# Two attention stages of a fused two-block kernel: heads taken in pairs on TensorE, and a longer distance between the steps of a head

## The reference

```
# latent attention (layer 0), 8 heads, q and k of 64+32 = 96 numbers, v of 64
s = (einsum('bhqd,bhkd->bhqk', qn, k_nope) + einsum('bhqr,bkr->bhqk', qr, k_rope)) * scale
p = softmax(s);  o = einsum('bhqk,bhke->bhqe', p, v)
# neighbourhood attention (layer 1), 16 heads, q, k, v of 64
s = einsum('bhcd,bhicjd->bhcij', q_row, k_win) * scale + bias
p = softmax(s);  o = einsum('bhcij,bhicje->bhce', p, v_win)
```

## Time and profile before

| what | value |
|---|---|
| median of 3 runs | 1599.57 us (1599.17 to 1601.21) |
| the profiled execution | 1597.99 us, of which span 1596.1 us |
| PE / DVE / ACT / POOL busy | 96% / 33% / 27% / 8% of the span |
| granted TensorE clock, mean | 0.986 of full speed |
| latent attention, first S to last out | 104.81 to 126.69 us |
| neighbourhood attention, first S to last out | 702.67 to 748.21 us |
| both experts' stretches | about 160 to 600 and 790 to 1230 us, DMA share 1.00 |

### The profile page before, as it was taken

One profiled execution on the slowest core, in us unless ns is written; L12 is line 12 of the kernel. 1 busy time (PEld: TensorE's weight loads), 2 busy tenths in 40 slices (PEclk: granted clock), 3 DMA queues, 4 the chain that ended last, 5 costly groups with the idle time before them and its releaser, 6 DMA issues.

```text
span 1596.1 us, 19750 instructions
## 1 busy us (share of the span) xinstructions
PE 1528.6 (96%) x8032; PEld 901.2 (56%) x8032; DVE 526.9 (33%) x1096; ACT 430.9 (27%) x730; POOL 132.5 (8%) x100
## 2 busy tenths in 40 slices
PE   7979999999999998999999999999999999899997
PEld 3554545454544445975544454544334596699986
DVE  1463311111111113035411111111111477578865
ACT  0251111111111112444111111111111461465554
POOL 0030100000000002842100000000000430000000
PEclk9999999999999999999999999999999999899999
DMA  9521999999999999731699999999999755445410
GB/s 338 196 95 67 399 427 428 429 427 427 428 428 428 429 429 384 267 162 51 263 400 426 429 429 427 427 427 427 429 429 381 273 211 204 166 160 206 163 53 27
DMA packets 69096, 502.50 MB, mean 315 GB/s; under 512 B 4000, under 2 KB 5280, under 8 KB 43552
## 3 DMA queue, kind: packets, MB, share of 16 engines
q1 hardware_dynamic: 68160, 495.17, 75.7%
q0 software_dynamic: 864, 6.29, 1.0%
HBM read 500.40 MB, written 1.05 MB: 314 GB/s over the span
## 4 chain that ended last, share of the span: by engine, by line
PE 81%; DMA 9%; DVE 5%; ACT 2%; issue 2%; SPq 0%; DVEq 0%; ACTq 0%
PE bank L853 25%; PE bank L877 11%; PE bank L1105 9%; DMA ring<-in_w_up 9%; PE bank L823 7%; PE bank L738 7%; PE bank L703 5%; PE bank L685 4%; PE bank L1116 4%; PE bank L837 3%; PE bank L808 2%; PE bank L785 1%; PE bank L797 1%; PE bank L863 1%; DMA ring<-in_w_in 1%
## 5 line engine op out<-in xcount | busy, mean ns | idle before, releaser
L853 PE MATMUL bank<-ring,arena 128*64 128x512 f32 x1536 | 343.9, 603 | 17.9 <-DMA ring<-in_w_up 9.9
L853 PEld LDWEIGHTS bank<-ring,arena 128*64 128x64 f32 x1536 | 114.0, 139 | 241.8 <-issue 241.6
L877 PE MATMUL bank<-ring,arena 128*64 128x512 f32 x768 | 170.1, 595 | 1.3 <-ACT arena L1239 1.3
L1655 DVE TENSOR_TENSOR arena<-arena,bank 128x512 f32<-128x512 f32 x32 | 22.0, 688 | 389.3 <-PE bank L853 389.3
L823 PEld LDWEIGHTS bank<-SEL,x_by_row 128*128 128x128 f32 x1088 | 124.0, 192 | 26.6 <-issue 26.0
L823 PE MATMUL bank<-SEL,x_by_row 128*128 128x128 f32 x1088 | 130.5, 278 | 0.3
L1667 DVE SCALAR_TENSOR_TENSOR y_low<-bank,ST,y_high 128x512 fp32r<-128x512 f32 x64 | 48.1, 751 | 201.2 <-ACT y_high L1243 201.2
L1105 PE MATMUL bank<-x_high,w_high 128*128 128x256 f32 x384 | 109.9, 286 | 2.6 <-DVE x_low L1497 2.6
L853 PE MATMUL bank<-arena 128*64 128x512 f32 x384 | 111.9, 592 | 0.0
L1243 ACT ACTIVATE y_high<-bank,ST 128x512 fp32r<-128x512 f32 x64 | 44.0, 687 | 248.1 <-PE bank L877 248.1
L877 PEld LDWEIGHTS bank<-ring,arena 128*64 128x64 f32 x768 | 53.9, 137 | 100.6 <-issue 100.6
(11 more groups left out here) (306 smaller groups left out, 2257.7 us busy)
## 6 DMA issues: line engine op xcount, KB each, us to landing
ring<-in_w_gate SPq DMA_DIRECT2D x48, 2048.0 KB, 19.5
ring<-in_w_up SPq DMA_DIRECT2D x48, 2048.0 KB, 20.0
ring<-in_w_down SPq DMA_DIRECT2D x48, 2048.0 KB, 18.0
arena<-in_w_gate SPq DMA_DIRECT2D x12, 2048.0 KB, 19.7
arena<-in_w_up SPq DMA_DIRECT2D x12, 2048.0 KB, 19.9
arena<-in_w_down SPq DMA_DIRECT2D x12, 2048.0 KB, 20.6
ring<-in_ffn_up SPq DMA_DIRECT2D x12, 2048.0 KB, 8.4
ring<-in_w_in SPq DMA_DIRECT2D x9, 2048.0 KB, 12.5
```

Source lines behind the costliest of these rows:

```text
L853: last = nc.tensor.matmul(bank[4 + m][64 * e:64 * e + 64, :], XG[:, c, 64 * e:64 * e + 64], w[e][:, c, :], start=(c == 0), stop=(c == C - 1))
L877: last = nc.tensor.matmul(bank[6 + half][64 * e:64 * e + 64, :], HT[:, j, 64 * e:64 * e + 64], w[e][:, j, 512 * half:512 * half + 512], st ...
```

## The change

The change rewrites the loops of both attention stages on PE, ACT and DVE. No instruction is added or dropped and none changes its size; order, waits and buffers differ. (The counts of PE are the same by kind, too.)

```diff
-                for i in range(n + 4):
-                    if i < n:
-                        a = a0 + i
-                        if i >= 3:
-                            pe.wait_ge(free, i - 2)
...
+                for i in range(n // 2 + 3):
+                    if i < n // 2:
+                        for a in (a0 + 2 * i, a0 + 2 * i + 1):
+                            if a - a0 >= 4:
+                                pe.wait_ge(free, a - a0 - 3 if free is a_free else a - 3)
+                            for t in range(T):
+                                last = nc.tensor.matmul(bank[4 + a % 4][:, t * SEQ:(t + 1) * SEQ], q(a - a0, t), k(a - a0),
+                                                        start=True, stop=True)
+                            last.then_inc(a_score, 1)
+                    if 0 <= i - 2 < n // 2:
+                        for a in (a0 + 2 * i - 4, a0 + 2 * i - 3):
+                            pe.wait_ge(a_p, a + 1)
...
+                            if a >= 2:
+                                pe.wait_ge(a_ptc, a - 1)
...
+                    if 0 <= i - 3 < n // 2:
+                        a = a0 + 2 * i - 6
                         pair = a // 2
-                        pe.wait_ge(a_ptc, a + 1)
-                        if a % 2 == 0 and pair >= 2:
+                        pe.wait_ge(a_ptc, a + 2)
+                        if pair >= 2:
                             pe.wait_ge(a_o, pair - 1)
                         for kt in range(T):
-                            last = nc.tensor.matmul(bank[2 + pair % 2][(a % 2) * 64:(a % 2) * 64 + 64, 0:SEQ],
-                                                    v(i - 4, kt), probs_t[a % 2][:, kt, :],
-                                                    start=(kt == 0), stop=(kt == T - 1))
+                            for e in range(2):
+                                last = nc.tensor.matmul(bank[2 + pair % 2][64 * e:64 * e + 64, 0:SEQ],
+                                                        v(a - a0 + e, kt), probs_t[e][:, kt, :],
+                                                        start=(kt == 0), stop=(kt == T - 1))
                         last.then_inc(a_pv, 1)
...
             def attention(a0, n, probs, probs_t, scale):
-                for i in range(n + 3):
-                    if i >= 3:
-                        a = a0 + i - 3
-                        act.wait_ge(a_pt, a + 1)
-                        if a >= 2:
-                            act.wait_ge(a_pv, a - 1)
...
+                for i in range(n + 4):
                     if i < n:
                         a = a0 + i
                         act.wait_ge(a_nb, a + 1)
-                        if a >= 4 and scale is not None:
+                        if i >= 4 and scale is not None:
                             act.wait_ge(a_pt, a - 3)
...
+                    if i >= 4:
+                        a = a0 + i - 4
+                        act.wait_ge(a_pt, a + 1)
+                        if a >= 2:
+                            act.wait_ge(a_pv, a // 2)
...
-            def continue_pair(i, a0, dest):
-
-                if i >= 5 and (i - 5) % 2 == 1:
-                    pair = (a0 + i - 5) // 2
-                    dve.wait_ge(a_pv, 2 * pair + 2)
+            def continue_pair(i, a0, n, dest):
+
+                if i >= 8 and i % 2 == 0 and i - 8 < n:
+                    pair = (a0 + i - 8) // 2
+                    dve.wait_ge(a_pv, pair + 1)
```

More of the change, by code:

```diff
@@ L777, in attention @@
             def attention(a0, n, q, k, v, probs, probs_t, free):
-                for i in range(n + 4):
-                    if i < n:
-                        a = a0 + i
-                        if i >= 3:
-                            pe.wait_ge(free, i - 2)
[L784 to L788, removed]
-                        a = a0 + i - 3
-                        pe.wait_ge(a_p, a + 1)
-                        if a0 == N_NA0:
-                            pe.wait_ge(a_p0, i - 2)
-                        if a >= 2:
[L794 to L802, removed]
@@ new lines, in attention @@
+                for i in range(n // 2 + 3):
[10 more added lines that the diff above has]
+                            pe.wait_ge(a_p, a + 1)
+                            if a0 == N_NA0:
+                                pe.wait_ge(a_p0, a - a0 + 1)
+                            if a >= 2:
+                                pe.wait_ge(a_ptc, a - 1)
+                            for t in range(T):
+                                for kt in range(T):
+                                    last = nc.tensor.transpose(
+                                        bank[a % 2][:, kt * SEQ + t * P:kt * SEQ + (t + 1) * P],
+                                        probs[a % 4][:, t, kt * P:(kt + 1) * P], ident)
+                            last.then_inc(a_pt, 1)
+                    if 0 <= i - 3 < n // 2:
+                        a = a0 + 2 * i - 6
@@ L1222, in attention @@
                         act.wait_ge(a_nb, a + 1)
-                        if a >= 4 and scale is not None:
+                        if i >= 4 and scale is not None:
                             act.wait_ge(a_pt, a - 3)
                         for t in range(T):
-                            src = bank[4 + a % 3][:, t * SEQ:(t + 1) * SEQ] if scale is not None else probs[a % 4][:, t, :]
+                            src = bank[4 + a % 4][:, t * SEQ:(t + 1) * SEQ] if scale is not None else probs[a % 4][:, t, :]
                             last = nc.scalar.activation(probs[a % 4][:, t, :], src, ACT.Exp, bias=nb[:, a % 4, t:t + 1],
@@ L1230, in attention @@
                         last.then_inc(a_exp, 1)
+                    if i >= 4:
[3 more added lines that the diff above has]
+                            act.wait_ge(a_pv, a // 2)
+                        nc.scalar.copy(probs_t[a % 2][:, :, :], bank[a % 2][:, :].rearrange("p (a b) -> p a b", b=SEQ))\
+                            .then_inc(a_ptc, 1)
             def experts(s, n, g):
@@ L1582, in normed @@
                 v.tensor_scalar(xn[:, t, :], X[:, t, :], rs_l[:, t:t + 1], None, ALU.mult).then_inc(xn_ready, 1)
-            def continue_pair(i, a0, dest):
-                if i >= 5 and (i - 5) % 2 == 1:
-                    pair = (a0 + i - 5) // 2
-                    dve.wait_ge(a_pv, 2 * pair + 2)
+            def continue_pair(i, a0, n, dest):
+                if i >= 8 and i % 2 == 0 and i - 8 < n:
+                    pair = (a0 + i - 8) // 2
+                    dve.wait_ge(a_pv, pair + 1)
                     v.tensor_copy(dest(pair - a0 // 2), bank[2 + pair % 2][:, 0:SEQ]).then_inc(a_o, 1)
             def attention(a0, n, probs, dest, scale, bias):
-                for i in range(n + 5):
+                for i in range(n + 7):
                     if i < n:
@@ L1624, in attention @@
                         last.then_inc(a_p, 1)
-                    continue_pair(i, a0, dest)
+                    continue_pair(i, a0, n, dest)
             def select(s, pair, g):
```

8 lines of the change are left out of this document (2 added, 6 removed).

## The result

| | before | after |
|---|---|---|
| median, lowest to highest | 1600.76 us, 1598.6 to 1601.75 (20 runs) | 1604.17 us, 1598.6 to 1610.4 (20 runs) |
| profiled execution, its span | 1597.99, 1596.1 | 1598.60, 1596.7 |
| mean granted clock | 0.986 | 0.980 |
| latent stage, first S to end of last out | 21.9 | 24.1 |
| neighbourhood stage, likewise | 45.5 | 46.3 |

What follows compares the result with a forecast made beforehand. PE was taken to bound the middle of both attention stages. Latent +0.8 and +1.2 for low clock, neighbourhood -1.0 with low clock, sum to +1.0 us on 1599.57: 1600.6. Forecast's own range 1597 to 1603, wider range 1595.5 to 1604.5.

Steps and rivals of the forecast that it cites:

- PE is no longer the bound: Both attention stages: overlapping halves cut PE's pair to 3.1 us from 5.3 (neighbourhood) and 3.8 from 5.0 (latent).
- The experts' stretch starts earlier or later as a whole.: Experts, paced by weight loads: they neither swallow nor add to what an attention stage gains, so stage changes count one for one.
- Latent stage +0.8 by the walk: Latent stage: longer start, with copy 0 behind exp 4, and a tail in pairs cost +0.8 us over eight heads.
- Latent stage +1.2 for low clock: Latent stage: gaps on PE bring one low-clock stretch, priced at 1.2 us, half of two.
- Neighbourhood middle 4.3 us a pair, a loop through the copy: Neighbourhood middle: a loop from V through softmax and copy takes 8.6 us for two pairs, 2.15 a head instead of 2.65.
- DVE's pace: Rival: loop closes faster, 2.0 us a head in the neighbourhood stage, latent stage equal; -5.0 us, 1594.6; chance 0.08.
- Neighbourhood stage, low clock +3.0 (two stretches): Neighbourhood stage: two low-clock stretches at 1.5 us each turn -4.0 into -1.0 us.
- low clock feeds itself: Part of the slower rival: a low stretch doubles PE's 3.1 us a pair, engines wait, the gap drops the clock again.
- slower rival: Low clock at three pairs or more, or row halves overlapping only from idle PE: +3.7 to +5.5 us; chance 0.22.
- within 0.2%: Whole kernel: change of at most 3.2 us either way, about what a measurement can tell; forecast chance 0.5, same overall 0.62.
- The clock holds: Rival: full clock everywhere and the loop runs as walked, -3.2 us, 1596.4; chance 0.2.
- Row halves that overlap only from an idle PE: Part of the slower rival: S costs 0.9 us more a pair and the walk's tail moves by +1.4.

Runs made afterwards that it cites:

- few-fillers kernel: Changed kernel plus one idle-time matmul of 256 columns ahead of each T in two or three turns at each stage's start: 1600.31 us, 0.9995 against before.
- many fillers: Changed kernel plus 49 idle-time matmuls of 256 columns ahead of T and, in the tail, V: 1607.96 us, 1.0035 against the kernel before.
- V head by head: Changed kernel with the matmuls of a pair's V in the order head, head instead of alternating: 1600.80 us in one execution.
- S in single heads: The best version with S of a pair's two heads apart again (S, T, S, T, V): 1596.15 us, 0.9967 against the kernel before.
- best version: Changed kernel with four buffers for transposed probabilities instead of two and copy of head i-3 ahead of exp i: 1585.88 us, 0.9909 against before.

## Why the prediction was right or wrong

- **"PE is no longer the bound", both overlaps carry over.** Right: S of a pair 1.14 us (1.2 forecast), V 1.08.
- **"The experts' stretch starts earlier or later as a whole."** Right. Its two lengths, 1.8 us apart, come without the change.
- **Latent stage +0.8 by the walk** (the prediction's programs followed head by head). Right in kind and size; its own figures give +0.7 against the trace of before and +1.0 against the walk of before. With the clock at 1.00 the few-fillers kernel has 22.36 us where the walk had 22.6 and the kernel before 21.9, and the slow links are those named: copy 0 behind exp 4, T 2 and T 3 behind copies 0 and 1, pairs in the tail. The first V came 0.8 us sooner than walked (11.6 after the first S, not 12.4).
- **Latent stage +1.2 for low clock.** One stretch was taken; the chip gave a double one of 6.8 us, from the first V on, in four of five executions of this code (24.1 to 24.6 us; 23.3 in the fifth, 1 us of which is the slow DVE instruction). From V to V it takes 4.80 and 3.85 us, where the few-fillers kernel has 3.87 and 2.97: +1.8.
- **Neighbourhood middle 4.3 us a pair, a loop through the copy.** The loop is what bounds it, and taking the copy out of it proved that (4.02 a pair afterwards). The size was 4.4 to 4.5: one round of a pair goes at DVE's pace (4.02), the next stands behind the copy (4.8 to 5.0). This makes the walk about 1 us short, as far as the profiles can tell. The first V came half a microsecond late (14.2, not 13.7), but that goes with low clock: with many fillers, at 1.00, it came after the 13.7 walked. The few-fillers kernel, which has one low stretch left, took 44.1 us, where walk plus one stretch is 41.5 + 1.5 = 43.0.
- **Neighbourhood stage, low clock +3.0 (two stretches).** This is the term that was too small, with the latent one. Three executions show 17, 20 and 31 us of low clock (part of the last in the projection), and stage lengths of 46.3, 48.3 and 50.4 us where 44.5 was forecast and 41 to 45.5 allowed; V head by head has 14 us and 45.0. I took two stretches of 3.4 us; their number and length differ from one execution to the next, and there are more of them: at the start for 10 us in two of the three, and in the tail, where every step waits for PE (last three V in 7.9 us instead of 5.3). That is the rival "low clock feeds itself", in part. Changed alone, though, the stage gave 45.4 us in its profile, with no low clock in its tail, and -1.0 us in the ratio, the number forecast: how far a profile lies above 44.5 differs from one execution to the next, and one profile can't average it.
- **The sum.** +3.7 (2.1 to 5.3) was measured, +1.0 forecast. The forecast was -3.2 at full clock and +4.2 for low clock. The few-fillers kernel stands at -0.8 (-2.7 to +1.1) with one stretch left in; without it (1.5) that is about -2.3 at full clock. So of the 2.7 us missed about 0.9 is the walk and about 1.8 the low clock, which costs some 6 us and not 4.2 (an estimate, each number good to 2 us, so this split is the likeliest and no more). The total is that of the slower rival (+3.7 to +5.5), of whose two causes only the clock was at work. That the forecast "within 0.2%" held was close: the median lies outside the forecast's own range (1597 to 1603) and 0.3 us inside the wider one, and 1.2 us of its distance from 1600.6 are the kernel before, whose median of 20 runs is 1600.76 and not 1599.57. What was left out altogether is the scatter: the median of the changed kernel lies 5.6 us over its profile, that of the kernel before 2.8.
- **Rivals.** "The clock holds" is nearly what the few-fillers kernel does, 0.9995 against before: even then next to nothing is won. "DVE's pace" needed the copy moved. Row halves that overlap only from an idle PE: wrong (1.14 us in the midst of the work).
- **The cause of low clock.** A low stretch behind a half-idle PE was the prediction's reading of one case, and it says that activity releases the low clock. S in single heads doesn't fit: PE was busy for 20.48 of 20.48 us at a granted clock of 0.50. What the few fillers show is that they took most of the low stretches away here, not by what rule.

The Trainium skill says that tiling speeds the matmuls and not the evacuation of PSUM, which may become the bottleneck (TensorEngine Tiling (Array Packing), "PSUM Bottleneck"). In the best version the bound did pass from PE to DVE, at 4.02 us a pair, but only 1.9 of these read PSUM (two times 0.75 for the scores, 0.42 for out); the rest is softmax work on SBUF. In the changed kernel the evacuation by ACT, the copy, is the bound too, but by its place in the order, not by its length of 0.58 us.

What stays open: how much four buffers alone would give the kernel before, which was not run; why the clock stays low under PE without a gap (S in single heads), and the 5.2 us ahead of the neighbourhood stage under many fillers. That the low clock accounts for the changed kernel's scatter is a correlation and two executions read in detail, not an experiment.

## What to carry to other kernels

A faster engine gives nothing as long as the loop goes through another: before deepening a pipeline, walk one item through all engines and ask behind which other item each of its steps now stands. Here one index (the copy of head i-4 behind exp i, not i-3), two buffers instead of four and the copy's place behind exp decided between +0.2% and -0.9%. With 8 or 16 items in a stage the fill and the tail weigh as much as the middle. And where the change leaves gaps on PE, look at the granted clock and at the scatter of the times, not only at one profile.

## What the runs showed of the hardware

- PE at 1.2 GHz for 20.48 us in which it was busy 20.48 us, with scores on 64 of 128 rows, transposes and value products (S in single heads). Being busy without a gap did not bring the full clock there.
- Row and column halves overlap when they stand back to back in PE's program, without alternating: 8 records in 1.14 and 1.09 us.
- The experts' stretch, bound by its loads, has two lengths 1.8 us apart (443.6 and 445.5 in the kernel before): 12 of the 28 stretches in the 14 profiles have the longer one, in the kernel before and in changed ones alike.
